# A decoder trunk: part of the next attention turn projected inside the attention core, wide value chunks, gate products in the MoE tail

## The reference

```python
h, gate = modulate(x, c, w_ada, b_ada)           # h = x * (1 + scale) + shift
# layer 0: 3 groups (window, dilation) = (128, 1), (512, 4), (2048, 16); 16 heads of 64
proj = (h @ w_in).reshape(B, S, 3, 3, 16, 64)    # group, (q, k, v), head, dim
q, k = rotary(proj[.., 0]) / 8, rotary(proj[.., 1]); v = proj[.., 2]
o_g, lse_g = dilated_window_attention(q, k, v, window, dil)   # for each group
o = sum_g softmax(lse)_g * o_g;  y = o @ w_out
x = layer_norm(ALPHA * x + gate * y) * ln_g + ln_b            # after every sub-layer
# layer 1
proj = h @ w_in                                   # q, k, v, z: 1024 columns each, then a, b: 8 each
qkv = silu(causal_depthwise_conv(proj[.., :3072], conv_w))
beta = sigmoid(b);  g = -exp(a_log) * softplus(a + dt_bias)
o = gated_delta_rule(q, k, v, g, beta);  y = (rms(o) * norm_w * silu(z)) @ w_out
```

## Time and profile before

| | |
|---|---|
| median of 3 runs | 2709.89 us (2707.2 to 2713.86) |
| profiled execution, device time | 2713.7 us |
| its span, first to last instruction | 2711.8 us |
| busy: PE | 2525.0 us, 93% |
| busy: PEld (weight loads) | 1377.0 us, 51% |
| busy: DVE, ACT, POOL | 1005.6 us, 672.4 us, 337.3 us |
| mean granted TensorE clock | 0.971 of full speed |
| attention stage, L675 | 768 records, 334.4 us busy, 596 ns mean |
| attention stage, L671 | 768 records, 176.5 us busy, 391 ns mean |

### The profile page before, as it was taken

One profiled execution on the slowest core, in us unless ns is written; L12 is line 12 of the kernel. 1 busy time (PEld: TensorE's weight loads), 2 busy tenths in 40 slices (PEclk: granted clock), 3 DMA queues, 4 the chain that ended last, 5 costly groups with the idle time before them and its releaser, 6 DMA issues. The chain is left out here.

```text
span 2711.8 us, 37865 instructions
## 1 busy us (share of the span) xinstructions
PE 2525.0 (93%) x13849; PEld 1377.0 (51%) x13850; DVE 1005.6 (37%) x2302; ACT 672.4 (25%) x1468; POOL 337.3 (12%) x390
## 2 busy tenths in 40 slices
PE   6999999999999999999996999999899999899995
PEld 2665656656764443333332476685774434333332
DVE  2444344433543322322207535446343332222217
ACT  1031030310312222222222433443312222222221
POOL 0101001010001111111100212122101111111110
PEclk9999999999999999999997999999999999999998
DMA  7624326252628999999965211312437999999966
GB/s 281 191 63 146 102 92 189 61 164 66 224 101 322 365 421 420 411 413 413 407 250 215 78 50 59 97 54 66 163 131 290 345 420 420 399 414 411 404 264 276
DMA packets 177815, 654.93 MB, mean 242 GB/s; under 512 B 26884, under 2 KB 88684, under 8 KB 122504
## 3 DMA queue, kind: packets, MB, share of 16 engines
q1 hardware_dynamic: 112752, 394.89, 37.4%
q10 hardware_dynamic: 29784, 149.13, 14.4%
q0 software_dynamic: 35136, 109.10, 11.5%
HBM read 614.18 MB, written 53.52 MB: 246 GB/s over the span
## 5 line engine op out<-in xcount | busy, mean ns | idle before, releaser
L1462 DVE TENSOR_SCALAR core_oT<-moe_tx,moe_by,moe_plus 128x128 f32<-128x128 f32 x360 | 123.0, 404 | 661.6 <-PE moe_tx L1709 661.4
L675 PE MATMUL attn_proj<-core_hT,core_ring 128*128 128x512 f32 x768 | 334.4, 596 | 8.5 <-ACTq L497 5.1
L1734 PE MATMUL moe_ph<-weights_w,core_oT 128*32 128x512 f32 (+2 forms) x1216 | 307.4, 615 | 8.8 <-issue 8.7
L1748 PE MATMUL moe_py<-weights_w,moe_hT 128*32 128x512 f32 (+2 forms) x1296 | 312.8, 596 | 0.9 <-ACT moe_hT L1186 0.9
L1734 PE MATMUL moe_pr<-weights_w,core_oT 128*64 128x512 f32 (+2 forms) x864 | 276.6, 604 | 10.7 <-issue 9.7
L675 PEld LDWEIGHTS attn_proj<-core_hT,core_ring 128*128 128x128 f32 x768 | 146.5, 191 | 188.9 <-issue 183.2
L2392 PE MATMUL gdn_pj<-core_hT,core_ring 128*128 128x512 f32 x512 | 226.8, 597 | 0.0
L1269 POOL DMA_INDIRECT y_rows<-moe_ysb,moe_yidx x90 | 93.6, 1040 | 951.2 <-ACT moe_ysb L1199 726.1
L1186 ACT COPY moe_hT<-moe_th 128x256 f32<-128x256 f32 x90 | 33.6, 374 | 659.2 <-PE moe_th L1697 659.2
L671 PE MATMUL attn_proj<-core_ring,core_hT 128*128 128x256 f32 x768 | 176.5, 391 | 0.0
L671 PEld LDWEIGHTS attn_proj<-core_ring,core_hT 128*128 128x128 f32 x768 | 169.3, 282 | 11.2 <-issue 3.8
(11 more groups left out here) (410 smaller groups left out, 3433.6 us busy)
## 6 DMA issues: line engine op xcount, KB each, us to landing
weights_w<-in_expert_w_dram SPq DMA_DIRECT2D x160, 1024.0 KB
weights_w<-in_expert_w_dram ACTq DMA_DIRECT2D x92, 1024.0 KB
core_ring<-in_expert_w_dram SPq DMA_DIRECT2D x54, 1024.0 KB
core_hT<-in_expert_w_dram SPq DMA_DIRECT2D x48, 1024.0 KB
core_ring<-in_attn_w_in_dram SPq DMA_DIRECT2D x36, 1024.0 KB, 7.4
weights_w<-y_rows SPq DMA_DIRECT2D x32, 1024.0 KB, 13.1
core_ring<-in_expert_w_dram ACTq DMA_DIRECT2D x30, 1024.0 KB
attn_ada_w<-in_ada_w_dram POOLq DMA_DIRECT2D x64, 384.0 KB, 5.8
```

The lines of the kernel that those rows point to most:

```text
L675: last = nc.tensor.matmul(proj[n % 2][:], w[:, j % SLOTS, kk, half_ * P:(half_ + 1) * P], c.hT[:, kk, :], start=kk == 0, stop=kk == KT - 1)
L1462: last = nc.vector.tensor_scalar(xT[:, b, k], tx[1][:, k - 4], by[:, k:k + 1], plus[:, k:k + 1], ALU.mult, ALU.add)
L1734: last = nc.tensor.matmul(ph[p % 2][at, :], xT[:, p % 2, k, at], w13[ew.up_place(n)[0]][:, :, k], start=k == 0, stop=k == KT - 1)
L1748: last = nc.tensor.matmul(py[n][at, :], hT2[:, p % 2, k, at], w2[ew.down_place(m)[0]][:, k, half(n)], start=k == 0, stop=k == 1)
```

## The change

In the attention stage the chunks stand in the order q, k, v of group 0, q, k of group 1, q, k of group 2, v of group 1, v of group 2. The last two are computed together: 512 moving columns from two ring slots. The first half (n = 0) of every turn is computed ahead: of the first before the loop, of the others in pieces inside the core of the turn before. `bank(n)` puts halves 0 and 1 both into `proj[0]`, so the core's `proj[1]` is not touched until half 2. The last turn stands outside the loop on PE and ACT. SP loads the ring's slots ahead of the row stores and issues the swap transfers of half 0. In the MoE tail of layer 0 the gate products are computed per tile, tokens stationary; the DeltaNet stage starts its projections at once, and its loop skips the first two in its first pass. The affine of `c.x` moves into the next MoE stage, and the load of that stage's ln rows waits for it.

```diff
 attention_stage
+    def bank(n):
+        return proj[(n + 1) % 2 if n else 0]
-    chunks = [(g, s) for g in range(GROUPS) for s in range(3)]
+    chunks = [(0, 0), (0, 1), (0, 2), (1, 0), (1, 1), (2, 0), (2, 1), (1, 2), (2, 2)]
+    PAIRED = 7
+    def used_up(n):
+        return 2 * (PAIRED + 2 if n >= PAIRED else n + 1)
 SP
             def turn(i, first):
-                ada.load_bias(sp, i)
                 for n, (g, s) in enumerate(chunks):
+                    if n == SLOTS:
+                        if not first:
+                            ada.store(sp, i - 1)
+                        ada.load_bias(sp, i)
+                        sp.wait_ge(proj_free, NPROJ * i + 3)
+                        for d in range(4):
+                            e = d ^ 1
+                            sp.dma_start(swp[32 * d:32 * d + 32, 0], raw[32 * e:32 * e + 32, 0]).then_inc(swp_in[0], 16)
                     if first and n < SLOTS:
                         continue
-                    sp.wait_ge(proj_done, NPROJ * i + 2 * n + 2)
+                    sp.wait_ge(proj_done, NPROJ * i + (used_up(n - SLOTS) + PC if n >= SLOTS else used_up(n + CH - SLOTS) - NPROJ + PC))
...
-                ada.store(sp, i)
+            ada.store(sp, QUADS - 1)
 ACT
+            def first_copy(i):
+                act.wait_ge(proj_done, NPROJ * i + 1 + PC)
+                act.wait_ge(rot_done, NROT * i + 1)
+                nc.scalar.copy(raw[:, 0], bank(0)[:]).then_inc(proj_free, 1)
+            def quad(i, following):
...
+                        if j >= PAIRED:
+                            nc.scalar.copy(v[:, 1:3, n - 2 * PAIRED, :],
+                                           bank(n)[:].rearrange("p (a f) -> p a f", f=QF)).then_inc(proj_free, 1)
...
                 for step in range(PAIRS + 3):
+                    if following and step == PAIRS + 2:
+                        first_copy(i + 1)
...
+            first_copy(0)
+            with act.Fori(0, QUADS - 1) as i:
+                quad(i, True)
+            quad(QUADS - 1, False)
 PE
+            def ahead(i, kks):
+                if kks[0] == 0:
+                    pe.wait_ge(w_in[0], 16 * (CH // SLOTS) * i + 16)
+                    pe.wait_ge(proj_free, NPROJ * i + 2)
+                for kk in kks:
+                    last = nc.tensor.matmul(bank(0)[:], w[:, 0, kk, 0:P], c.hT[:, kk, :], start=kk == 0, stop=kk == KT - 1)
+                if kks[-1] == KT - 1:
+                    last.then_inc(proj_done, 1)
...
+                        pe.wait_ge(proj_free, NPROJ * i + (n + 1 if n > 1 else 3))
+                        if n == 2:
+                            pe.wait_ge(oT_ready, PAIRS * i + 1)
+                        if j >= PAIRED:
+                            t = n - 2 * PAIRED
+                            for kk in range(KT):
+                                last = nc.tensor.matmul(bank(n)[:].rearrange("p (a f) -> p a f", f=QF), c.hT[:, kk, t:SEQ:RES],
+                                                        w[:, PAIRED % SLOTS:PAIRED % SLOTS + 2, kk], start=kk == 0, stop=kk == KT - 1)
...
                 ada.total(pe, i, 1, side)
+                if following:
+                    ahead(i + 1, (0, 1))
...
+                    if following and step == 0:
+                        ahead(i + 1, (2, 3))
                     if step < PAIRS:
                         turn(step, 0)
+                    if following and step < 2:
+                        ahead(i + 1, (4 + step,))
+                    if step < PAIRS:
                         turn(step, 1)
-                pe.wait_ge(oT_ready, PAIRS * (i + 1) + 1)
+                    if following and step in (PAIRS - 1, PAIRS):
+                        ahead(i + 1, (step - 1,))
+            ahead(0, range(KT))
+            with pe.Fori(0, QUADS - 1) as i:
+                quad(i, True)
+            quad(QUADS - 1, False)
 moe_stage
+                sp.dma_start(c.wab[:], delta_gates(A)).then_inc(wab_in, 16)        # not final, ahead of the wait for the order
+            if l:                                                                  # ACT, ahead of the ln row loads
+                act.wait_ge(x_before, 2 * TT)
+            if l:                                                                  # DVE, ahead of out_half(0, 0)
+                for row, op in ((0, ALU.mult), (1, ALU.add)):
+                    for t in range(TT):
+                        if row:
+                            dve.wait_ge(x_before, t + 1)
+                        nc.vector.tensor_tensor(c.x[:, t], c.x[:, t], c.ada[:, row], op).then_inc(x_before, 1)
+            def gates_of(t):                                                       # PE
+                pe.wait_ge(wab_in, 16); pe.wait_ge(laid2_act, t + 1); pe.wait_ge(laid2_dve, t + 1)
+                for k in range(KT):
+                    last = nc.tensor.matmul(pi[:, t * 2 * GH:(t + 1) * 2 * GH], c.hT[:, k, t * P:(t + 1) * P], c.wab[:, k],
+                                            start=k == 0, stop=k == KT - 1)
+                last.then_inc(ab_done, 1)
+                if t >= 2 and not final:                                           # behind the diagonal sums of tile t
+                    gates_of(t - 2)
                 if t and not final:
                     turn_next(t - 1)
             if not final:
+                gates_of(TT - 2)
                 turn_next(TT - 1)
+                gates_of(TT - 1)                                                   # then ACT copies pi to c.ab
 delta_stage
-            (gate load, product, copy, transposes; the affine of c.x on DVE)
+            pe.sem_inc(proj_done, 4)
+            pe.wait_ge(w_in[0], 16)
+            project(0, 0, 0)
             (transpose of the conv weights, cumulative products)
+            project(1, 0, 0)
-                proj(0), proj(1)
+                with pe.If(0 < i):
+                    proj(0), proj(1)
```

More of the change, by code:

```diff
@@ L143, in alloc_core @@
     c.upper = sb("upper", [P, P])
+    c.wab = sb("wab", [P, KT, 2 * GH])
+    c.ab = sb("ab", [P, TT, 2 * GH])
     return c
@@ L670, in _ @@
                                 for kk in range(KT):
-                                    last = nc.tensor.matmul(proj[n % 2][:, t % 2 * QF:(t % 2 + 1) * QF],
+                                    last = nc.tensor.matmul(bank(n)[:, t % 2 * QF:(t % 2 + 1) * QF],
                                                             c.hT[:, kk, toks], w[:, j % SLOTS, kk], start=kk == 0, stop=kk == KT - 1)
@@ L674, in _ @@
                             for kk in range(KT):
-                                last = nc.tensor.matmul(proj[n % 2][:], w[:, j % SLOTS, kk, half_ * P:(half_ + 1) * P],
+                                last = nc.tensor.matmul(bank(n)[:], w[:, j % SLOTS, kk, half_ * P:(half_ + 1) * P],
                                                         c.hT[:, kk, :], start=kk == 0, stop=kk == KT - 1)
@@ L1244, in _ @@
                 act.wait_ge(laid2_act, TT)
+                act.wait_ge(ab_done, TT)
+                nc.scalar.copy(c.ab[:], pi[:, 0:TT * 2 * GH].rearrange("p (t n) -> p t n", t=TT)).then_inc(ab_kept, 1)
+                act.wait_ge(ab_kept, 1)
             act.wait_ge(xn2_ready, TT)
@@ L2092, in _ @@
             act.sem_inc(proj_free, 2)
-            act.wait_ge(ab_done, 1)
-            nc.scalar.copy(abT, pre[0][0:2 * GH, :]).then_inc(ab_copied, 1)
-            act.wait_ge(ab_turned, 1)
-            abv = pre[1][:, 0:2 * TH].rearrange("p (t n) -> p t n", t=TT)
-            nc.scalar.activation(tab[:, BE], abv[:, :, GH:2 * GH], ACT.Sigmoid).then_inc(act_small, 1)
+            nc.scalar.activation(tab[:, BE], c.ab[:, :, GH:2 * GH], ACT.Sigmoid).then_inc(act_small, 1)
             act.wait_ge(small_in, 64)
@@ L2219, in _ @@
             ada.credits(dve)
-            for row, op in ((0, ALU.mult), (1, ALU.add)):
-                for t in range(TT):
-                    ch.do(nc.vector.tensor_tensor(c.x[:, t], c.x[:, t], c.ada[:, row], op))
-                ch.sync()
             ch.do(nc.vector.memset(raw[:, :, 0:CONV - 1], 0.0))
@@ L2364, in turn, with project @@
                 last.then_inc(done, 1)
-            pe.wait_ge(abw_in, 16)
-            for k in range(KT):
-                last = nc.tensor.matmul(pre[0][0:2 * GH, :], wab[:, k], c.hT[:, k], start=k == 0, stop=k == KT - 1)
-            last.then_inc(ab_done, 1)
-            pe.wait_ge(ab_copied, 1)
-            for t in range(TT):
-                last = nc.tensor.transpose(pre[1][:, t * 2 * GH:(t + 1) * 2 * GH], abT[:, t * P:(t + 1) * P],
-                                           c.ident[0:2 * GH, 0:2 * GH])
-            last.then_inc(ab_turned, 1)
+            def project(m, slot, i):
+                pe.wait_ge(proj_free, 2 * KINDS * i + m + 1)
+                for k in range(KT):
+                    last = nc.tensor.matmul(pj[m % 2][:], w[:, slot, k, m % 2 * P:(m % 2 + 1) * P], c.hT[:, k], start=k == 0, stop=k == KT - 1)
+                last.then_inc(proj_done, 1)
```

(8 more changed lines are left out.)

51 lines of the change are left out of this document (30 added, 21 removed).

## The result

The changed kernel took 2662.9 us in the median (2660.3 to 2666.2, 4 runs) where the kernel before took 2709.7 (2707.2 to 2713.9, 4 runs): a ratio of 0.9828, 95% interval 0.9813 to 0.9842. The prediction was 2665 (2652 to 2688).

| stretch, in us | before | after | gain |
|---|---|---|---|
| start to the ada total behind turn 1's projections | 171.86 | 170.16 | 1.7 |
| three turns, from that total to the one of turn 4 | 502.8 | 467.8 | 35.0 |
| last core, to the first product of the first MoE stage | 37.6 | 39.5 | -1.9 |
| first MoE stage, to DVE's first instruction of the next | 765.95 | 770.50 | -4.55 |
| from there to the first products for gc_row (behind DeltaNet's first two projections) | 37.19 | 19.65 | 17.5 |

What follows compares the result with a forecast made beforehand. PE was taken as the bound: its work, its standstills and lower-clock stretches. 10.0 + 17.7 + 6.7 - 2.0 - 5.9 + 19.2 - 0.8 - 0.3 = 44.6 us gained, so a median of 2665 us, range 2652 to 2688.

Steps and rivals of the forecast that it cites:

- Value chunks, 10.0: Attention projections: two 256-column value chunks as one 512-column set save 2.51 us a turn, 10.0 us in four turns.
- Gaps filled, 17.7: Attention cores: query-half pieces in PE's standstills save 5.9 us at each of three turn boundaries, 17.7 us.
- the clock in the core, 8.4 for three cores: Attention cores 1 to 3: with gaps filled the clock stays high, 2.8 us each, 8.4 us.
- The last core, -1.7: Last attention core, unfilled: its clock may fall, 0.6 x 2.8 = 1.7 us lost.
- First turn, -2.0: First attention turn: the second half shares the bank and must wait for ACT's copy, costing 2.0 us.
- Gates in the tail, -5.9: First MoE stage's tail: four gate sets cost 5.9 us: set 0 1.7, sets 1 and 2 nothing, set 3 3.8 plus 0.4.
- DeltaNet start, 19.2: Start of DeltaNet: first projection starts at once, 9.4 us cold; first two projections end after 18.1 instead of 37.35, gaining 19.2.
- Branch, -0.8; affine, -0.3: New branch in PE's DeltaNet loop costs 0.8 us; affine of x on DVE in the second MoE stage costs 0.3.
- (a): Attention cores: they stay at the lower clock, gain 27.5 us, total 2682; chance 0.20.
- (b): Attention cores: the DVE, ACT, PE loop bounds them, pieces delay it one for one, 17.7 us lost, 2683; chance 0.10.
- (c): Turn boundaries: ACT copies the first half late, standstill returns at each, 5.7 us lost, 2671; chance 0.05.
- (d): Paired value chunks: ring slot 2 arrives late, slower; a load landing at 29 us gives 2718 or more; chance 0.03.

Runs made afterwards that it cites:

- experiment 2: Changed kernel with one of the two halves of the paired value chunks back in 256-column form: 2668.5 us, ratio 0.9843 to the kernel before.
- Experiment 4: Changed kernel with all 8 products of the early query half in one place ahead of the core's first scores, none between transposes: 2679.5 us, ratio 0.988.
- experiment 5: Changed kernel with 7 dummy products of 256 columns in PE's standstills of the last attention core: 2662.8 us, ratio 0.9823.
- experiment 6: Changed kernel with gate sets 0 and 1 behind the sums of tile 3 and dummy products in the first MoE stage's tail: 2659.7 us, ratio 0.9818.
- experiment 1: Changed kernel with the paired value chunks back in 256-column form, 128 records a turn instead of 64: 2686.5 us, ratio 0.9913.
- experiments 1 and 3: The second is the changed kernel with all paired value chunks narrow and 223 instructions put ahead of PE's turn loop: 2691.3 us, ratio 0.9934.
- experiment 7: Changed kernel with dummy products in the first MoE stage's tail, gate set 0 left in place: 2659.2 us, ratio 0.9816; changed kernel beside it 2665.1 us.
- experiment 8: Changed kernel with ACT giving the bank credits for the first DeltaNet projection ahead of its six DMA issues: 2662.3 us, ratio 0.9819.

## Why the prediction was right, step by step

The total was right to 2 us: forecast gain 44.6, measured 46.8 between medians, 49.9 between the profiled executions, of which 2.1 lie in the second MoE stage, where no edit explains them. The terms were less exact than the sum, and its closeness is partly luck. Between the profiled executions, from which the terms are read, the gain was 5.3 us more than forecast. Misses of either sign stand in it (the DeltaNet start 1.7 too high; the core 1.8, the gates 1.4, branch and affine 1.1 and the first turn 0.9 too low), and the 2.1 us are less than the second MoE stage varies by itself. The range was wider than its working: its good end gave 2659, and no term leads to 2652.

- *Value chunks, 10.0.* Right: 1.2 us for half of the width (experiment 2), 2.4 a turn, 9.6. By the rule cited beside this term from the Trainium skill (SBUF — State Buffer, "Door 1: The DMA port swizzle") it would have been 1.3; the runs disagree with it.
- *Gaps filled, 17.7, and the clock in the core, 8.4 for three cores.* Right, together a little low: a turn went from 167.6 (mean of three) to 155.93 us, 11.7 less; without the width 9.3, against 5.9 + 2.8 = 8.7. Experiment 4 divides them. Of its 19.0 us, 10.6 are waits that came back (8.9 for probabilities, 1.7 at the last value products); the other 8.4 are put down to the clock, by subtraction.
- *The last core, -1.7.* A chance of 0.6 times 2.8 us. The fall came and cost 1.9; without it the term would have been nothing. In the traces here it came in 8 of 12 unfilled last cores (experiment 5).
- *First turn, -2.0.* Too dear: the standstill was 0.7 us, and 1.1 in all: the first row of the table gains 1.7 us, where the width (2.4) and an earlier start (41.09 instead of 41.51) would give 2.8. The 1.28 us of table load in the earlier trace rows did not come back ahead of the copy, which began at 50.89 us.
- *Gates in the tail, -5.9.* The stage says -4.55. The step that failed is set 0: its 1.7 us were taken as path, since PE is back to back up to the sums of tile 3. It cost 0.3 at most: where it is left out, PE waits 1.6 us at the same place for tile 1 to be normalised (experiment 6). In the kernel before that wait is not there (1448.16 us), and its trace alone could not show this; there PE had stood 3.40 us ahead of tile 0 and then run at a granted clock of 0.50 for 3.41 us. Set 3 with its copy was right: 4.0 us, from 2.32 to 6.33 between DVE's last work and the next stage, against 3.8 + 0.4. The last 0.2 us are less than the stage varies.
- *DeltaNet start, 19.2.* It was 17.5. The failed step is "the first projection starts at once": the credits stood behind six DMA issues of ACT, 2.5 us. In the kernel before, a DMA wait of 7.79 us had covered that. The cold projection took 9.87 us instead of 9.4, and the table was ready in time: 2.5 + 10.2 + 6.95 = 19.65 us from 1447.96 over 1450.47 and 1460.66 to 1467.61.
- *Branch, -0.8; affine, -0.3.* Both nothing: a DeltaNet turn took 109.1 us before and after, and PE reached the first turning of the second MoE stage 23.2 us after its first product there, 23.3 before.

The rivals: (a) is refuted by the clock of 1.00, which holds in the second and third core too (333 to 344 and 489 to 500 us); (b) by the steps, which keep 3.62 us from scores to scores once the pieces are past, all of it PE's own work; (c) by 207.45; (d) by the absence of any wait on the ring. Pieces stretched steps 0 and 1 to 6.13 and 3.61 us, under the 6.4 and 3.7 named. What the prediction did not have at all is the jump. The change writes the last turn out behind the loop and makes the body 128 instructions shorter; experiment 1 shows that the same design with a longer body would have cost 13 us more in that place. The turn loop of the kernel before showed no such standstill. Its expert stages do have waits for "issue":

```profile
PE moe_ph L1734 <- issue: 16.9, 5, 4.7
PE moe_pr L1734 <- issue: 9.7, 2, 5.1
```

No packet of q8 lies in any of these seven, so they are of another kind; what ends them is not shown.

## What to carry to other kernels

A short standstill in a dense stretch can be charged twice, once as itself and once as clock: look for work without inputs from the loop, cut it into pieces of the size of each gap, and put every piece into its gap rather than all of them ahead. When a wait is removed, list what had been hiding behind it on every engine (here six DMA issues ahead of a semaphore increment). And when a loop is rewritten, look at the first record behind each jump: a standstill put down to "issue", with packets on an instruction queue beside it, belongs to where the loop lies, not to what it computes. Without such packets "issue" says only that the profile does not know what ended the wait.

## What the runs showed of the hardware

- A jump back in PE's program costs 4.0 to 4.4 us of standstill in one layout and nothing in another with the same loop body (experiments 1 and 3); with the lower clock behind it, 5.7 and 7.4 us a jump.
- PE's clock fell in all three cores of experiment 4 behind standstills of 1.59 and 0.66 us, right after 7 us of dense work, and stayed at 0.54 over 18.5 us in the tail of the first MoE stage, where PE was busy for 8.1 (changed kernel, second trace); with dummy products in that tail it was 0.97 (experiment 7: 16 us, 11.6 busy). Slow records are not always a property of the record: in one trace of the changed kernel gate sets took 1.85 and 3.56 us.
- One DMA issue on ACT's queue took 2.00 us instead of 0.45 when PE began its projection at the same time (experiment 8, one trace).
